# First loads and first weight split of a fused encoder step in smaller pieces, with 16 throw-away products in place of 30

## The reference: what is computed

```python
h = x + 0.5 * swiglu(rmsnorm(x, g_ffn1), w1g, w1u, w1d)        # D_FF = 2816
u = rmsnorm(h, g_mix)
proj = u @ w_in                       # two groups of attention heads follow
h = h + concat([oa, ob]) @ w_out
h = h + 0.5 * swiglu(rmsnorm(h, g_ffn2), w2g, w2u, w2d)
y = rmsnorm(h, final_norm)
```

## Time and profile before

| | before |
|---|---|
| device time, median of 3 runs | 1053.2 us (1052.46 to 1053.62) |
| span of the profiled execution | 1050.4 us |
| PE busy | 1034.0 us (98%) |
| DVE busy | 805.4 us (77%) |
| ACT busy | 561.3 us (53%) |
| mean granted PE clock | 0.996 |

### The profile page before, as it was taken

How to read it: one execution, slowest core, us unless ns; L and a number is a source line. 1 busy time by engine, 2 the same in 40 slices (tenths; PEclk the granted TensorE clock), 3 DMA queues, 4 the chain that set the end, 5 groups by cost and what they waited for, 6 DMA issues and landing times. The chain is left out here.

```text
span 1050.4 us, 19614 instructions
## 1 busy us (share of the span) xinstructions
PE 1034.0 (98%) x7644; PEld 1001.7 (95%) x7644; DVE 805.4 (77%) x1259; ACT 561.3 (53%) x971; POOL 167.3 (16%) x296
## 2 busy tenths in 40 slices
PE   9999999999999999999999999999999999999996
PEld 9999999999999999988888889999999999999995
DVE  6998777788778994377757865798877788778894
ACT  7535644665546663344335544544654566555663
POOL 0000000000000055032444202200000000000023
PEclk9999999999999999999999999999999999999998
DMA  5435666566675435120112212416656666666532
GB/s 207 128 96 155 182 158 182 154 161 168 164 180 172 123 91 201 61 95 21 51 51 71 76 41 80 121 41 169 186 148 161 169 164 168 178 151 171 161 84 90
DMA packets 38506, 137.33 MB, mean 131 GB/s; under 512 B 4688, under 2 KB 8272, under 8 KB 38288
## 3 DMA queue, kind: packets, MB, share of 16 engines
q1 hardware_dynamic: 30352, 107.52, 29.8%
q0 software_dynamic: 8064, 28.58, 16.8%
HBM read 131.10 MB, written 4.98 MB: 130 GB/s over the span
## 5 line engine op out<-in xcount | busy, mean ns | idle before, releaser
L1765 DVE TENSOR_TENSOR w_lo<-raw,w_hi 128x1024 fp32r<-128x1024 f32 (+4 forms) x187 | 198.9, 1066 | 109.8 <-ACT w_hi L1280 93.4
L925 PE MATMUL acc<-c_hi,w_lo 128*128 128x288 f32 x952 | 282.0, 296 | 0.0
L925 PE MATMUL acc<-c_hi,w_hi 128*128 128x288 f32 x952 | 280.9, 295 | 0.0
L925 PE MATMUL acc<-c_lo,w_hi 128*128 128x288 f32 x952 | 277.6, 292 | 0.0
L1280 ACT ACTIVATE w_hi<-raw 128x1024 fp32r<-128x1024 f32 (+4 forms) x157 | 140.6, 897 | 80.4 <-PE acc L925 57.0
L1436 ACT ACTIVATE comb<-acc 128x288 f32<-128x288 f32 x224 | 92.1, 411 | 166.9 <-PE acc L925 164.6
L925 PEld LDWEIGHTS acc<-c_lo,w_hi 128*128 128x128 f32 x952 | 180.8, 190 | 0.0
L925 PEld LDWEIGHTS acc<-c_hi,w_hi 128*128 128x128 f32 x952 | 179.1, 188 | 0.0
L925 PEld LDWEIGHTS acc<-c_hi,w_lo 128*128 128x128 f32 x952 | 178.5, 188 | 0.0
L925 PE MATMUL acc<-h_hi,w_hi 128*128 128x288 f32 x574 | 170.7, 297 | 1.9 <-DVE h_lo L1898 0.8
L925 PE MATMUL acc<-h_hi,w_lo 128*128 128x288 f32 x574 | 169.9, 296 | 0.0
(11 more groups left out here) (257 smaller groups left out, 1858.9 us busy)
## 6 DMA issues: line engine op xcount, KB each, us to landing
raw<-in_w1st SPq DMA_DIRECT2D x17, 768.0 KB, 4.3
raw<-in_w2st SPq DMA_DIRECT2D x17, 768.0 KB, 4.2
raw<-in_w_qk SPq DMA_DIRECT2D x13, 512.0 KB, 3.8
raw<-in_w1sd SPq DMA_DIRECT2D x8, 768.0 KB, 4.2
raw<-in_w2sd SPq DMA_DIRECT2D x8, 768.0 KB, 4.3
raw<-in_w1gu SPq DMA_DIRECT2D x10, 512.0 KB, 4.5
raw<-in_w2gu SPq DMA_DIRECT2D x10, 512.0 KB, 3.9
raw<-in_w1st SPq DMA_DIRECT2D x9, 512.0 KB, 5.1
```

The source lines that it names most:

```text
L925: m = nc.tensor.matmul(acc[:, banks[side_of(p)], 0:HALF], w_part[:, col:col + P], x_part, start=n in (P1, P5, P2) and k == 0 and e == 0, s ...
L1765: return nc.vector.tensor_tensor(cols, src, hi.bitcast(FP32), ALU.subtract).then_inc(split_ready, 1)
```

## The change

The input tiles 0 and 1 are loaded by a transfer each (288 KB) in place of one for both (576 KB), and the first weight block by two transfers of half its columns (256 KB each, k-steps 0 to 3 and 4 to 7), in the order `x` 0, half 0, `x` 1, half 1. ACT and DVE split each half by itself, right behind the `hi` and `lo` of tiles 0 and 1. PE waits for the first half before k-step 0 and for the second before k-step 4. The first block counts as two groups, so all later counts grow by one. The products of ones become 16 in place of 30.

```diff
+FIRST_BLOCK = ("gu", 0, 0, 0)
...
-            place(("gu", ffn, f, 0), 1, 1)
+            place(("gu", ffn, f, 0), 2 if ("gu", ffn, f, 0) == FIRST_BLOCK else 1, 1)
...
-WARM_UP = 30
+WARM_UP = 16
...
-            for i in range(KD // 2):
-                sp.dma_start(res[:, 2 * i:2 * i + 2, :], a["x"][:, 2 * i:2 * i + 2, :]).then_inc(x_in[i], 16)
-                if i == 0:
-                    load_gate_up(0, 0, 0)
+            for i in range(2):
+                sp.dma_start(res[:, i, :], a["x"][:, i, :]).then_inc(x_in[i], 16)
+                at = raw_at(FIRST_BLOCK) + i * PART
+                sp.dma_start(raw[:, at:at + PART], a["w1gu"][0, :, 0, i * PART:(i + 1) * PART]).then_inc(
+                    raw_in[LANDING[FIRST_BLOCK][0]] if i else first_in, 16)
+            for i in range(1, KD // 2):
+                sp.dma_start(res[:, 2 * i:2 * i + 2, :], a["x"][:, 2 * i:2 * i + 2, :]).then_inc(x_in[i + 1], 16)
...
+                    if key == FIRST_BLOCK and k == KH:
+                        pe.wait_ge(split_ready, GROUP[key] + 2)
...
+            def hi_first(half):
+
+                if half:
+                    act.wait_ge(raw_in[LANDING[FIRST_BLOCK][0]], LANDING[FIRST_BLOCK][1])
+                else:
+                    act.wait_ge(first_in, 16)
+                base, at = split_base(FIRST_BLOCK) + half * PART, raw_at(FIRST_BLOCK) + half * PART
+                nc.scalar.activation(w_hi[:, base:base + PART], raw[:, at:at + PART], ACT.Copy).then_inc(hi_ready, 1)
+
             for d in range(KD):
-                act.wait_ge(x_in[d // 2], 16)
+                act.wait_ge(x_in[d if d < 2 else d // 2 + 1], 16)
                 u_hi_part(0, d)
-                if d == 0 or d == KD - 1:
-                    hi_block(("gu", 0, 0, min(d, 1)))
+                if d < 2:
+                    hi_first(d)
+                if d == KD - 1:
+                    hi_block(("gu", 0, 0, 1))
...
             for d in range(KD):
                 dve.wait_ge(uhi_ready, d + 1)
                 u_lo_part(0, d)
-                if d == 0 or d == KD - 1:
-                    lo_block(("gu", 0, 0, min(d, 1)))
+                if d < 2:
+                    base, at = split_base(FIRST_BLOCK) + d * PART, raw_at(FIRST_BLOCK) + d * PART
+                    lo_cols(w_lo[:, base:base + PART], raw[:, at:at + PART], w_hi[:, base:base + PART],
+                            GROUP[FIRST_BLOCK] + d)
+                if d == KD - 1:
+                    lo_block(("gu", 0, 0, 1))
```

More of the change, by code:

```diff
@@ L470, in hybrid_step @@
         NORM_BANK, FINAL_BANK, SPREAD_BANK, COPY_BANK = 6, 0, 2, 4
-        x_in = [sem(f"x_in{i}") for i in range(KD // 2)]
+        x_in = [sem(f"x_in{i}") for i in range(KD // 2 + 1)]
+        first_in = sem("first_in")
         gains_in = sem("gains_in")
```

## The result

| | before | after |
|---|---|---|
| device time, median of 10 runs | 1053.07 us | 1054.89 us (1054.05 to 1056.86) |
| ratio | | 1.0024 (95% interval 1.0015 to 1.0033) |
| span of the profiled execution | 1050.4 us | 1053.3 us |
| mean granted PE clock in it | 0.996 | 0.992 |

One run of before at 1428 us was disturbed and is not in the ratio. By the ratio the change makes the kernel slower by 0.24%, 2.5 us; the two medians are 1.8 us apart. The forecast was 1053.1 us, no change, with a range of 1052.0 to 1053.8 us, and the measured 1054.89 us lies above it.

The account below looks back on a forecast made before the run. PE, busy 1034.0 of 1050.4 us, bounds the kernel; early token sums also wait for transfers, ACT and DVE. Of 3.1 us won, 2.9 is given back, leaving 0.1: 1053.2 to 1053.1 us, range 1052.0 to 1053.8.

Parts of the forecast that it names:

- the load order leaves the landing of `x` 2 and 3 where it was: First loads: the pair lands at 8.36 us against 8.23 before, 0.13 us later for smaller rows.
- this landing decides, and not PE: At tile 2 ACT waits for the transfer, starting at 8.39 us; the token sums wait for the adds until 22.34 us.
- PE's earlier start is swallowed: Up to the token sums PE gives back 2.9 of 3.1 us in waits, 1.0 us of it before tile 2.
- Start of the products: After 16 products of ones, the first real product starts at 7.4 us instead of 10.47, 3.1 us earlier.
- Rival (c): Small rows slower at the cold start: pair lands 0.5 us later, token sums 0.35 us later, 1053.6 us; chance 0.07.
- The estimate by the Trainium skill: First 1.11 MB at about 240 GB/s for 256 KB transfers: 1.9 us slower, time some 1054.9 us.
- Rival (d): PE idles in pieces between 9 and 16 us, its clock falls to 1.2 GHz: 1058.7 us for one block; chance 0.04.
- The sum: Whole kernel: 3.1 us won at the start, 2.9 given back, 0.1 us left; median 1053.2 to 1053.1 us.
- a late or early start handed on unchanged: From the start to the end: a time won before the first real product is handed on nearly whole.

Follow-up runs that it names:

- e1: The kernel before with 16 products of ones in place of 30, loads unchanged; measured ratio 1.0002.
- e9: The kernel before with short cuts later in the queue: `x` 4 to 7 by a transfer each, second block in two halves of its columns; ratio 1.0007.
- e2: The changed kernel with its 30 products of ones put back, loads and splits as changed; measured ratio 1.0021.
- e6: The kernel before with 24 products of ones, token sums moved behind the third block's first k-step, spreading of the roots three k-steps later; ratio 1.0011.
- e11: The kernel before with 38 products of ones in place of 30, loads unchanged; measured ratio 1.0007.
- e12: The changed kernel once more, nothing altered, for a second profile; PE idle for 3.4 us, then at 1.2 GHz until 17.7 us.

## Why the prediction was wrong

- **That the load order leaves the landing of `x` 2 and 3 where it was** is the step that failed. I priced the short rows at 0.13 us (0 to 0.22), from the mean rate of a stretch late in the kernel, and got 8.36 us. Measured with the changed loads: 9.38, 10.23, 10.72 and 11.18 us. Two things are missing in the price. The engines as a whole moved less before 7 us, so that the middle one of the 16 pieces was 0.5 to 0.8 us late. And the last piece, for which the wait is, came 1.0 to 2.7 us behind the middle one, where it was 0.28 us in before. All of the 1.0 us that after lost at the start comes from this term.
- **That this landing decides, and not PE**, was right: ACT started tile 2 with an idle time ended by the transfer, at 9.41 us, and the token sums followed the landing as 22.42 + (landing - 8.38) in the runs. My forecast left 0.05 us of room (landing at 8.36, tile 2 wanted at 8.41 us): the kernel before has next to none between that landing (8.2 us) and its use (8.41 us), so nearly every tenth by which it slips is lost.
- **That PE's earlier start is swallowed** was right, and `e1` shows it alone: 1.38 us earlier, 0.2 us kept. The pieces were of other sizes in after: 2.07 us before tile 2, where I had 1.0.
- **Start of the products.** Forecast 7.4 us, measured 6.89 us; the clock rose at 4.9 us in that execution, not at 6.7. The durations of the halves, 0.63 and 0.68 us, came out as 0.63 and 0.69 us.
- **Rival (c)**, small rows that move slowly at the cold start, had 0.07 and a landing 0.5 us later. That part came true: 0.56 us by the rates up to 7 us, 0.46 us by the middle piece in after. What (c) lacks is the lag of the last piece, which makes up most of the delay and also comes when the engines are warm (`e9`). The estimate by the Trainium skill, page "DMA: Bandwidth & Descriptors", section "Bandwidth", came to 1054.9 us, which is the measured time, but by another way. It took 240 GB/s for the small transfers, where the trace has 302 between 4 and 7 us, and the late engine is not in it, so that the numbers meet is luck.
- **Rival (d)**, the clock, had 0.04. Its fall was seen in three of three profiles of the changed loads with 16 products; I had argued with gaps of 1.0 us, and the gap was 2.1 to 3.4 us, because the pair was late. It is not what makes the kernel slower: with 30 products (`e2`), where the clock did not fall at this place, the ratio is 1.0021 against 1.0024 and 1.0019.
- **The sum.** A late start of 1.0 us was measured in the profile, and the times differ by 1.8 us (medians) to 2.5 us (ratio). By the table the landing differs between executions and was later than in the first profile in the three others of these loads (10.2 to 11.2 us, 1.8 to 2.8 us by the law), which is enough for the size. In the executions that were not profiled the landing is not known, and the share of the falls of the clock cannot be had from single profiles. What is added at 370 us, where POOL meets DVE (0.6 us in after, 1.1 in `e2`, next to nothing in `e1`, `e6` and `e11`), was in no term of the prediction. It had a late or early start handed on unchanged.

## What to carry to other kernels

A wait for a transfer is a wait for the last of its 16 pieces: before cutting a transfer to get its first part sooner, look how much room the transfers queued behind it have before they are wanted, and price both the lower rate and the spread of the pieces, not a mean rate from another place. When two chains meet at one point within 0.2 us, shortening one gains 0.2 us at most, and any slip of the other is lost nearly in full. An idle gap of PE that the change opens may cost nothing in one execution and 1.5 us in the next.

## What the runs showed of the hardware that was not expected

- With rows of 2304 and 2048 bytes (and with two transfers with rows of 128 bytes) among the first loads, the last of the 16 pieces of a transfer behind or among them came 0.9 to 3.4 us after the first, in ten profiles. With rows of 4096 bytes and more over all partitions it was 0.45 to 0.72 us, in seven. The lag stays for the transfers queued behind (2.24, 2.27, 2.27 us in `e12`). Why an engine falls back, and which, the traces do not say.
- Transfers over 64 partitions moved 248 GB/s at full share in the place where 361 were moved over 128.
- A DVE instruction with two inputs took up to 1.3 us longer when it met an addition on POOL (1.79 us in place of 0.55).
- The clock fell for 3.4 to 6.9 us behind waits of PE of 0.6 to 3.4 us, in eight of the fourteen profiles that had one in the first 26 us.
